# Gate-scaled expert rows added onto the token rows in scratch memory; the last item returned by one-hot matmuls

## The reference, cut to what matters

```python
def moe_swiglu(h, w_router, b_router, w_gate, w_up, w_down):
    t = h.reshape(-1, shp[-1])
    logits = (t @ w_router).astype(jnp.float32)
    _, top_idx = lax.top_k(logits + b_router, TOP_K)                 # TOP_K = 2 of 8
    top_w = jax.nn.softmax(take_along_axis(logits, top_idx), -1)
    gates = sum(one_hot(top_idx, 8) * top_w[..., None], axis=1)
    out = zeros_like(t)
    for e in range(8):
        out = out + gates[:, e:e + 1] * swiglu(t, w_gate[e], w_up[e], w_down[e])
...
x = x + moe_swiglu(rmsnorm(x, g_ffn), ...)
y = rmsnorm(x, g_final)                                              # D_MODEL 1024, D_FF 2816
```

## Time and profile before

| What | Value |
|---|---|
| median of three runs | 1456.08 us (1453.92 to 1458.16) |
| the profiled execution | 1455.75 us, span 1453.9 us |
| PE busy | 1359.0 us (93%) |
| DVE busy | 950.0 us (65%) |
| ACT busy | 786.9 us (54%) |
| POOL busy | 78.1 us (5%) |
| granted PE clock, mean | 0.964 of 2.4 GHz |
| first transposes of the first item | at 647.5 us |
| last matmul of the last item starts | at 1425.4 us |

### The profile page before, as it was taken

The page is one execution under the profiler, slowest core; times in us unless marked ns, Lnnn a source line. Parts: engine busy times, 40 slices in busy tenths (PEclk is TensorE's granted clock), DMA queues, the critical chain, the costliest instruction groups (busy, mean ns, idle before and its releaser), DMA issues.

```text
span 1453.9 us, 19177 instructions
## 1 busy us (share of the span) xinstructions
PE 1359.0 (93%) x6856; PEld 1116.3 (77%) x6856; DVE 950.0 (65%) x906; ACT 786.9 (54%) x776; POOL 78.1 (5%) x111
## 2 busy tenths in 40 slices
PE   5899999989979999959999999999999999999982
PEld 4789899978667777547888888888888888888871
DVE  2533333455446454247888888888888888888883
ACT  1423332334445233126777777777777777777761
POOL 1000000002200000010001001010010000100001
PEclk9899999999969999969999999999999999999996
DMA  8543525221210422467999999999999999999924
GB/s 267 184 145 116 168 96 168 76 97 50 54 47 1 154 72 53 155 242 279 370 360 375 381 372 387 364 366 395 362 379 377 360 395 363 374 383 367 382 101 127
DMA packets 136563, 354.99 MB, mean 244 GB/s; under 512 B 18282, under 2 KB 54458, under 8 KB 136177
## 3 DMA queue, kind: packets, MB, share of 16 engines
q1 hardware_dynamic: 133337, 343.72, 65.5%
q0 software_dynamic: 3184, 10.71, 2.0%
HBM read 346.73 MB, written 7.82 MB: 244 GB/s over the span
## 4 chain that ended last, share of the span: by engine, by line
PE 85%; SPq 4%; DVE 3%; issue 2%; ACT 2%; DMA 2%; POOL 1%; ACTq 0%; DVEq 0%; POOLq 0%
PE PS L1452 24%; PE PS L1453 24%; PE PS L1454 24%; PE PS L1722 2%; SPq L523 1%; PE PS L1855 1%; SPq L519 1%; SPq L521 1%; PE PS L1477 1%; PE PS L1466 1%; PE PS L1791 1%; PE PS L1618 1%; PE PS L1702 1%; PE PS L1628 1%; PE PS L1848 1%
## 5 line engine op out<-in xcount | busy, mean ns | idle before, releaser
L987 DVE TENSOR_TENSOR LOW<-RAW,UH 128x2048 fp32r<-128x2048 f32 x275 | 628.4, 2291 | 155.6 <-ACT UH L684 155.6
L684 ACT CAST UH<-RAW 128x2048 fp32r<-128x2048 f32 x275 | 526.1, 1914 | 254.7 <-PE PS L1454 254.7
L1452 PE MATMUL PS<-UH,XH 128*128 128x512 f32 (+1 forms) x768 | 292.9, 381 | 1.4 <-DVE XL L1349 1.4
L1454 PE MATMUL PS<-UH,XL 128*128 128x512 f32 (+1 forms) x768 | 290.9, 379 | 0.0
L1453 PE MATMUL PS<-LOW,XH 128*128 128x512 f32 (+1 forms) x768 | 290.9, 379 | 0.0
L1452 PEld LDWEIGHTS PS<-UH,XH 128*128 128x128 f32 x768 | 145.7, 190 | 30.6 <-DVE XL L1349 1.8
L1454 PEld LDWEIGHTS PS<-UH,XL 128*128 128x128 f32 x768 | 145.5, 190 | 29.3
L1453 PEld LDWEIGHTS PS<-LOW,XH 128*128 128x128 f32 x768 | 145.7, 190 | 29.0
L1452 PE MATMUL PS<-UH,ATH 128*128 128x512 f32 x352 | 139.2, 395 | 4.7 <-DVE ATL L1365 4.7
L1453 PE MATMUL PS<-LOW,ATH 128*128 128x512 f32 x352 | 138.4, 393 | 0.0
L1454 PE MATMUL PS<-UH,ATL 128*128 128x512 f32 x352 | 138.0, 392 | 0.0
(11 more groups left out here) (276 smaller groups left out, 1609.5 us busy)
## 6 DMA issues: line engine op xcount, KB each, us to landing
RAW<-in_moe_w_down SPq DMA_DIRECT2D x88, 1024.0 KB, 5.1
RAW<-in_moe_w_gate SPq DMA_DIRECT2D x64, 1024.0 KB, 5.1
RAW<-in_moe_w_up SPq DMA_DIRECT2D x64, 1024.0 KB, 5.1
RAW<-in_moe_w_gate SPq DMA_DIRECT2D x24, 768.0 KB, 6.3
RAW<-in_moe_w_up SPq DMA_DIRECT2D x24, 768.0 KB, 6.7
PAIR<-in_ffn_w_gate SPq DMA_DIRECT2D x11, 1024.0 KB, 5.4
PAIR<-in_ffn_w_up SPq DMA_DIRECT2D x11, 1024.0 KB, 7.9
RAW<-in_ffn_w_down SPq DMA_DIRECT2D x11, 1024.0 KB, 5.0
```

The costliest lines, as they stand in the source:

```text
L684: nc.scalar.copy(dst, src).then_inc(unit_high, 1)
L987: V_.tensor_tensor(dst, src, high.bitcast(F32), ALU.subtract).then_inc(unit_low, 1)
L1452: mm(out, wh, xh, start=start, stop=False, skip_group_check=True)
L1454: return mm(out, wl, xh, start=False, stop=stop, skip_group_check=True)
```

## The change

- The sum over a token's two experts moves into the transfers. A second scratch tensor `tokens_added` (`XD`) gets a copy of `X` before the first item. For every item but the last, ACT multiplies the rows by their gates while it copies them out of PS (`GC`, one number for each row), and POOL's indirect store adds them to the token's row (`compute_op=ALU.add`). Rows of an item that hold no token go to 128 rows of `XD` in front of the tokens, so no row is named twice.
- The last item does not go through memory. ACT writes its scaled rows rounded (`YH`), DVE the rest (`YL`), and PE brings them back to token order by matmuls with a one-hot matrix `BACK[:, t, :]` (12 matmuls, two for each tile and half). SP loads `X` from `XD` while the last item still runs. DVE adds one PS result to each tile.
- In the last item the turning of chunk 2 stands before the fourth down unit of chunk 1 and no longer behind it, on PE, ACT and DVE alike, and the last unit finishes one half of the columns before the other.
- The gates of each row are made early: seven DVE instructions between two `LOW` of the first item, and 12 small matmuls (14 columns) behind the `FIRST` units. The one-hot product for `IDX` has half the columns. Semaphores are merged.

```diff
@@ POOL, before the first item
+                    t = MIXED[k]
                     pool.wait_ge(normed[3], k + 1)
-                    pool.dma_start(HND[MIXED[k] * TT:(MIXED[k] + 1) * TT, :], HN[:, MIXED[k], :]).then_inc(y_stored, 16)
+                    pool.dma_start(HND[1 + t * TT:1 + (t + 1) * TT, :], HN[:, t, :]).then_inc(y_stored, 16)
+                    pool.dma_start(XD[CAP + t * TT:CAP + (t + 1) * TT, :], X[:, t, :]).then_inc(y_stored, 16)
+                    if k == 0:
+                        pool.dma_start(HND[0:1, :], HN[0:1, t, :]).then_inc(y_stored, 16)
+                        pool.dma_start(XD[0:TT, :], HN[:, t, :]).then_inc(y_stored, 16)
+                        pool.dma_start(XD[TT:CAP, :], HN[0:CAP - TT, t, :]).then_inc(y_stored, 16)
         pool.wait_ge(i_idx, 1)
-        pool.wait_ge(y_stored, 16 * NT)
+        pool.wait_ge(y_stored, TOKENS_STORED)
...
@@ POOL, in the loop over items
-            pool.indirect_dma_start(YD, bass.IndirectOffsetOnAxis(IDXY[:, 0:1], 0), YS[:, :], None).then_inc(y_stored, 16)
-        pool.wait_ge(y_stored, 16 * before_last + 16 * NT)
-        pool.wait_ge(i_y, 2 * before_last + 4)
-        nc.gpsimd.tensor_copy(IDXY[:, :], IDX[:, 1, :][:, bass.ds(before_last, 1)]).then_inc(pool_step, 1)
...
-        pool.indirect_dma_start(YD, bass.IndirectOffsetOnAxis(IDXY[:, 0:1], 0), YS[:, :], None).then_inc(y_last, 16)
+            pool.indirect_dma_start(XD, bass.IndirectOffsetOnAxis(IDXY[:, 0:1], 0), YS[:, :], None, compute_op=ALU.add)\
+                .then_inc(y_stored, 16)
@@ ACT, item
+                if last and i == DN0:
+                    act.wait_ge(y_stored, 16 * j + TOKENS_STORED)
...
-                elif i == GU0 - 1:
+                elif i == (GU0 - 2 if last else GU0 - 1):
                     hidden_high(2, j)
...
-                nc.scalar.copy(YS[:, h * 512:(h + 1) * 512], PS[:, 4 + h, :]).then_inc(i_y, 1)
+                if h == 0 or last:
+                    act.wait_ge(back_half, h + 1) if last else act.wait_ge(unit_used, NU * (j + 1) + NF + len(order))
+                nc.scalar.activation((YH if last else YS)[:, h * 512:(h + 1) * 512], PS[:, 4 + h, :], ACT.Copy,
+                                     scale=GC[:, 0:1]).then_inc(i_y, 1)
@@ DVE, after the last item
-            link(V_.scalar_tensor_tensor(out=X[:, t, :], in0=YG[t][:, 0, :], scalar=RC[:, 6, t:t + 1], in1=X[:, t, :], ...
-            V_.scalar_tensor_tensor(out=X[:, t, :], in0=YG[t][:, 1, :], scalar=RC[:, 7, t:t + 1], in1=X[:, t, :],
+        for h in range(2):
+            dve.wait_ge(i_y, 2 * before_last + 3 + h)
+            V_.scalar_tensor_tensor(out=YL[:, cols], in0=PS[:, 4 + h, :], scalar=GC[:, 0:1], in1=YH[:, cols].bitcast(F32),
+                                    op0=ALU.mult, op1=ALU.subtract).then_inc(back_ready, 1)
+            dve.wait_ge(x_back, 16 * NT)
+            dve.wait_ge(back_mm, t + 1)
+            V_.tensor_tensor(X[:, t, :], X[:, t, :], PS[0:TT, back_bank(t):back_bank(t) + 2, :]..., ALU.add)
@@ PE, behind the FIRST units, and after the last item
+        pe.wait_ge(diag_made, 3)
+        for v in range(2):
+            for n in range(2 * NT):
+                ins = mm(PS[:, 5, 0:MAXI + 1], OB[:, n, :], MG[:, v, n, :], ...)
...
+            units(j, order, GU0, GU0 + 2)
+            for h in range(2):
+                for i in range(2):
+                    ins = three(PS[:, 4 + h, :], ATH[:, 4 + i, :], ATL[:, 4 + i, :], UH[n % HIGH][:, cols], ...)
+                ins.then_inc(back_half, 1)
...
+        for t in range(NT):
+            for h in range(2):
+                mm(PS[0:TT, back_bank(t) + h, :], BACK[:, t, :], YH[:, cols], start=True, stop=False, ...)
+                ins = mm(PS[0:TT, back_bank(t) + h, :], BACK[:, t, :], YL[:, cols], start=False, stop=True, ...)
+            ins.then_inc(back_mm, 1)
@@ SP, after the last weight load
-        sp.wait_ge(y_last, 16)
         for t in range(NT):
-            sp.dma_start(YG[t][:, :, :].rearrange("p i d -> p (i d)"), rows).then_inc(y_in[t], 16)
+            sp.wait_ge(unit_used, NU * (before_last + 1) + NF + GU2)
+            sp.dma_start(X[:, t, :], XD[CAP + t * TT:CAP + (t + 1) * TT, :]).then_inc(x_back, 16)
```

More of the change, by code:

```diff
@@ L69 @@
 RING = 11
+TOKENS_STORED = 16 * (2 * NT + 3)
 HIGH = 3
@@ L148, in shape_constants @@
     put("iota", np.tile(np.arange(P), (P, 1)))
-    put("part", np.arange(P)[:, None])
+    put("part", np.arange(P)[:, None] - (CAP - 1))
     r = np.arange(P)[:, None]
@@ L1381, in _ @@
         V_.tensor_tensor(RC[:, 4:6, :], RC[:, 10:12, :], RC[:, 0:1, :].to_broadcast([TT, 2, NT]), ALU.subtract).then_inc(r_dve, 1)
-        for n in range(NF):
+        low_first(HIGH)
+        dve.wait_ge(r_act, 1)
+        link(V_.tensor_tensor(rc(10), rc(6), rc(7), ALU.add))
+        link(V_.reciprocal(rc(11), rc(10)))
+        link(V_.tensor_tensor(GF[:, :, :], RC[:, 6:8, :], RC[:, 11:12, :].to_broadcast([TT, 2, NT]), ALU.mult))
+        link(V_.tensor_copy(GH[:, :, :], GF[:, :, :]))
+        link(V_.tensor_tensor(GF[:, :, :], GF[:, :, :], GH[:, :, :].bitcast(F32), ALU.subtract))
+        for v, part in enumerate((GH[:, :, :].bitcast(F32), GF[:, :, :])):
+            ins = V_.tensor_tensor(MG[:, v, :, :], OA[:, :, :], part.rearrange("p i t -> p (i t)").unsqueeze(2)
+                                   .to_broadcast([TT, 2 * NT, MAXI + 1]), ALU.mult)
+        ins.then_inc(diag_made, 1)
+        for n in range(1, NF):
             if n == NF - 1:
@@ L1385, in _ @@
             low_first(n + HIGH) if n + HIGH < NF else split(0, n + HIGH - NF)
+        dve.wait_ge(r_cnt_mm, 3)
+        link(V_.tensor_copy(GT[:, :], PS[:, 5, 0:MAXI]))
+        link(V_.tensor_scalar(IS0[:, :], IDX[:, 0:MAXI], 0.0, cn("part"), ALU.is_equal, ALU.mult))
+        V_.scalar_tensor_tensor(out=IDS[:, :], in0=IDX[:, 0:MAXI], scalar=float(CAP - 1), in1=IS0[:, :], op0=ALU.add, op1=ALU.add)\
+          .then_inc(i_idx, 1)
         def item(j, last):
@@ L1898, in item @@
                 turn_tokens(j + 1)
-            units(j, order, DN1, GU0)
+            units(j, order, DN1, GU0 - 1 if last else GU0)
             if not last:
@@ L1902, in item @@
             turn_hidden(2, j)
+            units(j, order, GU0 - 1 if last else GU0, DN2 if not last else GU0)
+            pe.wait_ge(i_atl, 6 * j + 6)
             if not last:
-                units(j, order, GU0, DN2)
-            pe.wait_ge(i_atl, 6 * j + 6)
-            units(j, order, len(order) - 3, len(order))
+                units(j, order, DN2, NU)
+                return
+            units(j, order, GU0, GU0 + 2)
+            n = NF + GU0 + 2
+            pe.wait_ge(unit_low, NU * (j + 1) + n + 1)
+            for h in range(2):
+                for i in range(2):
+                    cols = slice((2 * i + h) * 512, (2 * i + h + 1) * 512)
+                    ins = three(PS[:, 4 + h, :], ATH[:, 4 + i, :], ATL[:, 4 + i, :], UH[n % HIGH][:, cols],
+                                LOWS[n % RING][:, cols], False, i == 1)
+                ins.then_inc(back_half, 1)
         with pe.Fori(0, before_last) as j:
@@ L1910, in _, with back_bank @@
         item(before_last, True)
+        pe.wait_ge(back_ready, 1 + NT)
+        for t in range(NT):
+            for h in range(2):
+                if t == 0:
+                    pe.wait_ge(back_ready, 1 + NT + h + 1)
+                cols = slice(h * 512, h * 512 + 512)
+                mm(PS[0:TT, back_bank(t) + h, :], BACK[:, t, :], YH[:, cols], start=True, stop=False, skip_group_check=True)
+                ins = mm(PS[0:TT, back_bank(t) + h, :], BACK[:, t, :], YL[:, cols], start=False, stop=True, skip_group_check=True)
+            ins.then_inc(back_mm, 1)
     ctx.close()
+def back_bank(t):
+    return (0, 2, 6)[t]
 def key_bank(p):
```

97 lines of the change are left out of this document (54 added, 43 removed).

## The result

The changed kernel takes 1439.27 us (median of four runs, 1439.03 to 1440.23) against 1457.12 in the same comparison: ratio 0.9878, 95% interval 0.9861 to 0.9895. The forecast was 1438.1. Its profiled execution took 1439.03 us with a span of 1437.20, 16.72 less than before.

The account below looks back on a forecast made before the run. PE bounds the middle items, the chain of waits the end; 2.7 + 2.9 + 12.4 = 18.0 us, in front 0, takes the profiled 1455.75 to 1437.7, median 1438.1; 8 in 10: 1434.5 to 1444.

Parts of the forecast that it names:

- Turning and clock: Last item: turning one unit earlier cuts PE's idle time, gain 2.7 us; PE's clock then stays up, 2.9 us.
- rival 1: Last item: PE's clock falls all the same, wholly or partly; price 1.7 to 2.9 us, chance 0.18.
- From the last matmul to the first addition: End of last item: return by matmuls takes 2.3 us instead of 11.1; gain 8.8, at least 8.1.
- Additions and norm: Kernel end: one addition a tile instead of two; copy to last norm end 12.2 us, with the return gaining 12.4.
- In front: Before the first item: added stores, gate instructions and small matmuls cost 0 us net.
- the first gather moves: Sign in front that the prediction is wrong; the first gather was expected at 642 to 643 us.
- rival 2: In front: the first gather waits for the added stores; price 1.1 us, 5 if weights go first; chance 0.06.
- The loop: Middle items: PE is full and its list unchanged, so 0 us; an item stays at 95.1 us.
- The adding store: Loop and last item: it may take four times as long as the plain store unseen; 0 us, own time estimated 4.4.
- Rival 3: All items: slow adding store holds up weights beyond some 15 us reserve each, 21 in the last; chance 0.05.
- Rival 4: Last unit: PE's return no shorter because DVE or ACT stand in each other's way; some 3 us, chance 0.05.

Follow-up runs that it names:

- experiment 7: The changed kernel with plain indirect stores in place of the adding ones: 1436.33 us (0.986).
- experiments 5 and 6: 5: kernel before with buffers 32 bytes lower, at the changed kernel's addresses, 1453.8 us (0.9984); 6: changed kernel at the old addresses, 1437.55 us in one run.
- experiment 2: The changed kernel with the last item returned through scratch memory by the adding store, without return matmuls or additions after it: 1444.54 us (0.9925).
- experiment 10: The changed kernel with twelve more plain 512 KB stores of YS behind each adding store: 1505.92 us.

## Why the prediction was right, step by step

- **Turning and clock** (2.7 + 2.9): 2.76 of idle time and 2.8 of clock in the profiled pair, and 5.5 in the turning alone. That the clock stays up behind 1.9 us is usual and not certain: rival 1 came true in experiment 7, for 1.55 us, a little under its price of 1.7 to 2.9; one execution in six had it, and it had a chance of 0.18.
- **From the last matmul to the first addition** (8.8): 8.7. The handovers and half copies were a little dearer (copy 0.69, `YL` 0.75) and cancel in part.
- **Additions and norm** (together 12.4): 12.95 by the table, 12.9 from copy to norm end. POOL's second root instruction took 0.57 for every tile, as forecast (1.57 and 1.46 before for the first two), though the first one took 1.06 for the second tile. The third addition ended at 8.2 after the copy (8.45 forecast), its root at 10.4 (10.9) and the last norm at 11.7 (12.2).
- **In front** (0): the sum missed +3.9, and the test "the first gather moves" struck, at 646.86. The mechanism that I had priced there, the gather waiting for stores (rival 2), did not occur: `IDX` released it, 5.5 us after the last added store had landed. What the term left out is PE's clock: 2.8 of the 3.9 are two falls, in a stretch whose list of instructions is the same as before, and at least the first goes with the moved addresses (experiments 5 and 6). If that is its cause, which is not shown, the two misses here and in the loop are of one kind. The twelve small matmuls regained nothing: the clock fell behind them too (0.51).
- **The loop** (0): that the change "leaves PE's list in the loop as it was" was true and not enough. A matmul's length depends on the addresses of its tiles, and the shorter table moved them: -1.7 (experiments 5 and 6). I had counted the table's columns only as work for DVE and PE.
- **The adding store** (0 seen): right, 6.4 to 9.7 us under 95. For its time alone, the estimate from the Trainium skill's "DMA: Bandwidth & Descriptors" ("Anatomy of one DMA") was 4.4; the trace of experiment 2 has 6.39, and that decides.
- **Rival 3** did not come, but its price was wrong in the loop: experiment 10 shows no reserve of 15 us for each item. Its price for the last item came out about right there.
- **Rival 4** did not come: PE waits 0.51 for the second `YL`, as counted.

So in the profiled pair 18.57 at the end, 1.7 in the items and 0.4 between stand against 3.9 in front: 16.7. The medians differ by 17.85. That this is so near the forecast's 18.0 is luck: the terms that it had at nothing cancel in part, and the other 1.1 lies within what the front changes from one execution to the next. The gain at the end, 18.57 against 18.0, is not luck.

## What to carry to other kernels

Work out each end of the chain by its own rows: here idle time, clock and transfers at the end came out within 0.6 us. Compare two traces by stretches between the same events before believing a total, because a front that varies by 7 us can hide a term of 5. And where a change shifts buffers, even by 32 bytes, look at the mean length of the unchanged matmuls, and at their clock, in every stage.

## What the hardware showed that was not expected

- **The distance between a matmul's stationary and moving tile matters.** With `XH` at a multiple of 4096 bytes from `UH`, 390 ns and items of 93.7; 32 bytes beyond one, 94.9; 384 short of one, 94.85; 416 short, 95.12. `ATH` stands at a multiple in all kernels, and its matmuls take 390 in all. Why, and which other distances are free, is open: only these were tried.
- **The clock in front differs where PE's list does not.** One and the same list of matmuls at 604 to 622 us ran at 1.00 in one profiled execution and at 0.50 for two stretches of it in the other; the first of these falls is in all ten profiled executions with the buffers 32 bytes lower and in none of the four others. The execution matters too: runs of the kernel before with a mean granted clock of 0.966 took 1452.75 to 1453.58, with 0.959 to 0.960 they took 1456.15 to 1460.87, and no trace of such a run was kept.
- **An adding indirect store costs twice a plain one** when alone (6.39 against 3.32), and 1.7 us more beside weight loads (6.8 against 5.1). Its issue holds POOL for 1.60 us instead of 1.01 (experiments 6 and 5).
